# Two reorderings in a 36,612-instruction kernel: weight sums inside a recurrent step, and how an attention's key and value weights are cut into chunks

## The reference, cut to what matters

```
scores = einsum('bhtk,bhsk,bhtsk->bhts', qc, kc, decay)
out    = (qc * exp(b)) @ state + scores @ vc
state  = exp(b_last) * state + (kc * exp(b_last - b)).T @ vc
```

```
kv = (kv_lat @ w_kvb).reshape(T, 6, 128 + 128)
k_nope = rms_norm(kv[..., :128], kn_w);  v = kv[..., 128:]
q_nope = rms_norm(q[..., :128], qn_w);   q_pe = rms_norm(q[..., 128:], ...)
```

## Time and profile before

| | us |
|---|---|
| median of 3 runs | 2535.42 |
| lowest, highest run | 2530.89, 2548.64 |
| profiled execution: its own time | 2550.24 |
| profiled execution: span of the core | 2548.5 |
| mean granted TensorE clock in it | 0.959 of full |
| PE busy | 2434.4 (96%) |
| ACT, DVE, POOL busy | 882.3, 980.6, 932.2 |
| recurrence, round 0 and round 1 (from first scores to last modulation sums) | 139.1 to 236.5, 337.0 to 432.8 |
| stage `kvb` | 1251.9 to 1345.9 |

### The profile page before, as it was taken

The page is one execution under the profiler, slowest core; times in us unless marked ns, Lnnn a source line. Parts: engine busy times, 40 slices in busy tenths (PEclk is TensorE's granted clock), DMA queues, the critical chain, the costliest instruction groups (busy, mean ns, idle before and its releaser), DMA issues.

```text
span 2548.5 us, 36612 instructions
## 1 busy us (share of the span) xinstructions
PE 2434.4 (96%) x14273; PEld 2020.4 (79%) x14273; DVE 980.6 (38%) x1667; ACT 882.3 (35%) x1359; POOL 932.2 (37%) x794
## 2 busy tenths in 40 slices
PE   6999998999999999999999999999999999999997
PEld 3866876988888888888896778888887886688766
DVE  4772673344323223434213235222324004752173
ACT  5433333324222223335212344222344225633462
POOL 2463364233233232334321115444565441135302
PEclk8999899999999999999867999999999999999999
DMA  7177168211222222213100002333332321122211
GB/s 281 59 275 270 50 244 335 63 58 50 66 61 62 66 59 65 66 58 100 43 21 1 1 17 83 99 99 94 95 92 101 109 97 56 52 67 85 71 49 66
DMA packets 56953, 234.94 MB, mean 92 GB/s; under 512 B 6336, under 2 KB 7616, under 8 KB 56064
## 3 DMA queue, kind: packets, MB, share of 16 engines
q1 hardware_dynamic: 56592, 232.45, 27.2%
q0 software_dynamic: 240, 0.79, 0.1%
HBM read 231.11 MB, written 2.10 MB: 92 GB/s over the span
## 4 chain that ended last, share of the span: by engine, by line
PE 82%; DMA 4%; DVE 4%; POOL 3%; ACT 3%; issue 3%; SPq 0%; DVEq 0%; POOLq 0%; ACTq 0%
PE ps L854 15%; PE ps L855 15%; PE ps L856 15%; PE ps L1503 4%; PE ps L1505 4%; PE ps L1506 4%; DMA XB<-ada_dram 4%; PE ps L607 2%; PE ps L1393 2%; POOL w_low L464 2%; PE ps L1319 1%; PE ps L1720 1%; PE ps L1733 1%; PE ps L1657 1%; PE ps L894 1%
## 5 line engine op out<-in xcount | busy, mean ns | idle before, releaser
L464 POOL TENSOR_TENSOR w_low<-ring,w_high 128x512 fp32r<-128x512 f32 (+2 forms) x534 | 696.1, 1326 | 1237.3 <-ACT w_high L455 1228.4
L455 ACT ACTIVATE w_high<-ring 128x1024 fp32r<-128x1024 f32 (+2 forms) x267 | 274.6, 1031 | 973.8 <-PE ps L856 626.2
L854 PE MATMUL ps<-h_high,w_high 128*128 128x512 f32 x1040 | 410.3, 394 | 14.9 <-POOL h_low L717 7.0
L855 PE MATMUL ps<-h_low,w_high 128*128 128x512 f32 x1040 | 407.1, 391 | 0.0
L856 PE MATMUL ps<-h_high,w_low 128*128 128x512 f32 x1040 | 406.4, 391 | 0.0
L854 PEld LDWEIGHTS ps<-h_high,w_high 128*128 128x128 f32 x1040 | 196.6, 189 | 61.9 <-POOL h_low L717 12.9
L856 PEld LDWEIGHTS ps<-h_high,w_low 128*128 128x128 f32 x1040 | 196.4, 189 | 41.6
L855 PEld LDWEIGHTS ps<-h_low,w_high 128*128 128x128 f32 x1040 | 196.8, 189 | 38.3
L1503 PE MATMUL ps<-hidden,w_high 128*128 128x512 f32 (+1 forms) x504 | 178.6, 354 | 0.0
L1505 PE MATMUL ps<-hidden,w_high 128*128 128x512 f32 (+1 forms) x504 | 178.5, 354 | 0.0
L1506 PE MATMUL ps<-hidden,w_low 128*128 128x512 f32 (+1 forms) x504 | 178.3, 354 | 0.0
(11 more groups left out here) (463 smaller groups left out, 5091.3 us busy)
## 6 DMA issues: line engine op xcount, KB each, us to landing
XB<-ada_dram SPq DMA_DIRECT2D x84, 768.0 KB, 6.6
ring<-up_dram SPq DMA_DIRECT2D x88, 512.0 KB, 3.6
ring<-down_dram SPq DMA_DIRECT2D x44, 512.0 KB, 3.6
ring<-winE_dram SPq DMA_DIRECT2D x32, 512.0 KB, 3.3
ring<-win_dram SPq DMA_DIRECT2D x20, 512.0 KB, 3.6
ring<-winC_dram SPq DMA_DIRECT2D x20, 512.0 KB, 3.3
arena<-ada_dram SPq DMA_DIRECT2D x12, 768.0 KB, 20.7
XB<-xl_dram SPq DMA_DIRECT2D x2, 2048.0 KB, 9.1
```

Of the source, the lines that this page charges most:

```text
L455: nc.scalar.activation(WH[p][:, 0:L], RAW[p][:, 0:L], ACT.Copy).then_inc(w_hi, 1)
L464: ins = nc.gpsimd.tensor_tensor(WL[p][:, to], RAW[p][:, to], WH[p][:, to].bitcast(F32), ALU.subtract)
L854: nc.tensor.matmul(bank[:, 0:n], wh[:, cols], hi, start=(k == 0), stop=False)
L855: nc.tensor.matmul(bank[:, 0:n], wh[:, cols], lo, start=False, stop=False)
```

## The change

In the recurrence the order on PE is different. The first two levels of `scores(n)` come first, then `mod_sums(g)`, then levels 2, 3, the transposes and the last level, then `mod_sums(g+1)`, then `outputs(n-1)` directly followed by `updates(n)`, `mod_turn(g-1)` and `mod_sums(g+2)`. The number of instructions is the same.

In stage `kvb` a chunk holds either the keys of two heads or the values of two heads (256 columns for each half of the latent), in turn. For an even h PE does the keys of heads h and h+1 (24 products with 512 or 256 moving tokens); for an odd h it does the values of heads h-1 and h, 36 products with 256 moving columns in place of 72 with 128, two token tiles to a bank. The sums are counted anew (`key_sum`; 7 per pair in place of 8). The means that stood between the token tiles stand all together behind each chunk, the spreads behind them as before. ACT copies four key sums behind each even chunk, DVE three value sums behind each odd one; POOL's waits for the keys follow the new count.

```
--- before.py
+++ after.py
@@ -97,7 +97,7 @@
 
 LAST_SUM = dict(
     win0=lambda k: 2 * k + 1 if k < 6 else 14 + 2 * (k - 7), win1=lambda k: 2 * k + 1 if k < 6 else 14 + 2 * (k - 7),
-    wmlp=lambda k: (1, 3, 6, 6, 9, 9, 11, 13)[k], wout0=lambda k: 2 * k + 1, winM=lambda k: k if k < 5 else 2 * k - 4, qb=lambda k: k, kvb=lambda k: 4 * k + 3,
+    wmlp=lambda k: (1, 3, 6, 6, 9, 9, 11, 13)[k], wout0=lambda k: 2 * k + 1, winM=lambda k: k if k < 5 else 2 * k - 4, qb=lambda k: k, kvb=lambda k: 7 * (k // 2) + (6 if k % 2 else 3),
     woutM=lambda k: k, winE=lambda k: k, woutE=lambda k: 2 * (k - 3) + 1 if k < 6 else k, winC=lambda k: k, woutC=lambda k: k,
 )
 
@@ -106,7 +106,7 @@
     win1=(19, B5), hgS1=(30, B5), hgK1=(13, (5,)), hgU1=(12, (6,)), ro1=(5, (5, 6)),
     wmlp=(14, B5), sv=(8, B8), wout0=(16, B8),
     n1=(4, B8), up0=(88, B8), down0=(12, B8),
-    n2=(4, (5, 6)), n2d=(2, (7, 4)), winM=(11, B5), nlat=(7, (5, 6, 7)), qb=(9, B8), ropek=(1, (7,)), kvb=(24, B5), nqkM=(2, (5,)), nqk=(21, (6, 7)),
+    n2=(4, (5, 6)), n2d=(2, (7, 4)), winM=(11, B5), nlat=(7, (5, 6, 7)), qb=(9, B8), ropek=(1, (7,)), kvb=(21, B5), nqkM=(2, (5,)), nqk=(21, (6, 7)),
     fa=(4, (0, 1, 2, 3)), ropeq=(3, (0, 1, 2)), fb=(2, (3, 4)),
     mS=(24, (0, 2)), mT=(24, (4,)), mV=(6, (6,)), mL=(6, (7,)), woutM=(8, B8),
     n3=(2, (6, 7)), n3d=(2, (4, 5)), up1=(44, (0, 1, 2, 3)), down1=(8, B8),
@@ -857,7 +857,7 @@
                 sums_done(ins, sums, g + i)
             return g + len(segs)
 
-        def split_tokens(pe, stage, c, sums, g, kt, width, m0, src, groups, between=None):
+        def split_tokens(pe, stage, c, sums, g, kt, width, m0, src, groups):
 
             wh, wl = await_parts(pe, stage, c)
             for group in groups:
@@ -870,10 +870,7 @@
                         nc.tensor.matmul(to, hi, wh[:, cols], start=(k == 0), stop=False)
                         nc.tensor.matmul(to, lo, wh[:, cols], start=False, stop=False)
                         ins = nc.tensor.matmul(to, hi, wl[:, cols], start=False, stop=(k == kt - 1))
-                    if t == group[-1]:
-                        sums_done(ins, sums, g)
-                    if between:
-                        between(t)
+                sums_done(ins, sums, g)
                 g += 1
             return g
 
@@ -1096,6 +1093,9 @@
         NM, LSUM, LINV, SKX = carve((2, 4, 2), (2, 4, 2), (2, 4, 2), (2, 4, 2), at=ARENA - 4 * P)
         YM = HL
         qk_hi, qk_lo = sem("qk_hi"), sem("qk_lo")
+
+        def key_sum(h, s):
+            return 7 * (h // 2) + 2 * (h % 2) + s
 
         M_PARTED = [("r", 0), ("k", 0), ("q", 0), ("t", 0), ("k", 1), ("q", 1), ("t", 1), ("k", 2), ("q", 2), ("k", 3), ("q", 3),
                     ("t", 2), ("k", 4), ("q", 4), ("k", 5), ("q", 5)]
@@ -1374,11 +1374,12 @@
                 for c in range(2, 10):
                     win_chunk(r, c)
 
-                def scores(n):
+                def scores(n, levels):
 
                     w = n % 2
-                    pe.wait_ge(hg_ops, 2 * (6 * r + n) + 1)
-                    for l in range(NL + 1):
+                    if levels[0] == 0:
+                        pe.wait_ge(hg_ops, 2 * (6 * r + n) + 1)
+                    for l in levels:
                         if l == NL:
                             pe.wait_ge(hg_ops, 2 * (6 * r + n) + 2)
                             bank = open_bank(pe, SK, keys_sum(n)).rearrange("p (h c t) -> p h c t", h=2, c=2)
@@ -1425,11 +1426,13 @@
                 for n in range(7):
                     g = step_mods(r, n)
                     if n < 6:
-                        scores(n)
+                        scores(n, range(NL // 2))
                     mod_sums(g)
+                    if n < 6:
+                        scores(n, range(NL // 2, NL + 1))
+                    mod_sums(g + 1)
                     if n:
                         outputs(n - 1)
-                    mod_sums(g + 1)
                     if n < 6:
                         updates(n)
                     if n:
@@ -1576,17 +1579,35 @@
             pe.wait_ge(m_tab, 32)
             pe.wait_ge(lat_lo, 4)
             sums_done(nc.tensor.matmul(bank[:, :], C("rot"), M_PE[:, 0, 0:S], start=True, stop=True), "ropek", 0)
-            def mean_behind(h, t):
-                behind = {2: (3, 5), 3: (1, 3, 5), 4: (1, 3, 4, 5)}[len(QK_MEANS[h])]
-                if t in behind:
-                    mean(pe, "nqk", QK_MEANS[h][behind.index(t)])
-
             for h in range(6):
-                g = split_features(pe, "kvb", h, "kvb", 4 * h, 2, 2 * P,
-                                   lambda s, k: (seg_of(KVH, k, s), seg_of(KVL, k, s)), (0, 1))
-                split_tokens(pe, "kvb", h, "kvb", g, 2, 2 * P, P,
-                             lambda t, k: (KVH[:, k, t * P:(t + 1) * P], KVL[:, k, t * P:(t + 1) * P]),
-                             (range(4), range(4, 6)), lambda t: mean_behind(h, t))
+                wh, wl = await_parts(pe, "kvb", h)
+                MM = nc.tensor.matmul
+                if h % 2 == 0:
+                    for j in range(2):
+                        for s, (_, n) in enumerate(SEGS):
+                            bank = open_bank(pe, "kvb", key_sum(h + j, s))[:, 0:n]
+                            for k in range(2):
+                                hi, lo = seg_of(KVH, k, s), seg_of(KVL, k, s)
+                                cols = slice((2 * k + j) * P, (2 * k + j + 1) * P)
+                                MM(bank, wh[:, cols], hi, start=(k == 0), stop=False)
+                                MM(bank, wh[:, cols], lo, start=False, stop=False)
+                                ins = MM(bank, wl[:, cols], hi, start=False, stop=(k == 1))
+                            sums_done(ins, "kvb", key_sum(h + j, s))
+                else:
+                    for t in range(6):
+                        g = 7 * (h // 2) + 4 + t // 2
+                        bank = bank_ap("kvb", g) if t % 2 else open_bank(pe, "kvb", g)
+                        to = bank[:, t % 2 * 2 * P:(t % 2 + 1) * 2 * P]
+                        for k in range(2):
+                            hi, lo = (x[:, k, t * P:(t + 1) * P] for x in (KVH, KVL))
+                            cols = slice(2 * k * P, 2 * (k + 1) * P)
+                            MM(to, hi, wh[:, cols], start=(k == 0), stop=False)
+                            MM(to, lo, wh[:, cols], start=False, stop=False)
+                            ins = MM(to, hi, wl[:, cols], start=False, stop=(k == 1))
+                        if t % 2:
+                            sums_done(ins, "kvb", g)
+                for k in QK_MEANS[h]:
+                    mean(pe, "nqk", k)
                 for k in QK_SPREADS[h]:
                     spread(pe, "nqk", k)
             for k in QK_MEANS[6]:
@@ -2130,9 +2151,10 @@
                 if h == 3:
                     root("nqk", 0)
                 ahead("kvb", h)
-                for s in range(2):
-                    bank = await_sums(act, "kvb", 4 * h + s)
-                    taken(A(seg_of(M_KN, h, s), bank[:, 0:SEGS[s][1]], ACT.Copy), "kvb", 4 * h + s)
+                for x in () if h % 2 else (h, h + 1):
+                    for s in range(2):
+                        bank = await_sums(act, "kvb", key_sum(x, s))
+                        taken(A(seg_of(M_KN, x, s), bank[:, 0:SEGS[s][1]], ACT.Copy), "kvb", key_sum(x, s))
             root("nqk", 1)
             for t in range(4):
                 bank = await_sums(act, "fa", t)
@@ -2368,11 +2390,11 @@
                     for c in range(2, 6):
                         for k in QK_MEANS[c - 2]:
                             if k >= 9:
-                                await_taken(pool, "kvb", 4 * ((k - 9) // 2) + (k - 9) % 2)
+                                await_taken(pool, "kvb", key_sum(*divmod(k - 9, 2)))
                             pool_square("nqk", k, 0)
                         split_lo(stage, c)
                     for k in range(11, 21):
-                        await_taken(pool, "kvb", 4 * ((k - 9) // 2) + (k - 9) % 2)
+                        await_taken(pool, "kvb", key_sum(*divmod(k - 9, 2)))
                         pool_square("nqk", k, 0)
                     for x in range(len(M_PARTED)):
                         whole, high, low_ = m_parts(*M_PARTED[x])
@@ -2773,11 +2795,11 @@
             await_taken(dve, *spread_sum("nlat", 3))
             rotate("ropek", 0, M_PE[:, 0, 0:S], 0)
             for h in range(6):
-                for x, (a, b) in enumerate(((0, 4), (4, 6))):
-                    g = 4 * h + 2 + x
+                for x in range(3 if h % 2 else 0):
+                    g = 7 * (h // 2) + 4 + x
                     bank = await_sums(dve, "kvb", g)
-                    taken(nc.vector.tensor_copy(M_V[:, a:b, h, :],
-                                                bank[:, 0:(b - a) * P].rearrange("p (t n) -> p t n", n=P)), "kvb", g)
+                    taken(nc.vector.tensor_copy(M_V[:, 2 * x:2 * x + 2, h - 1:h + 1, :],
```

(4 more changed lines are left out.)

## The result

| | before | after |
|---|---|---|
| median, runs on the same chip | 2542.53 (9 runs, 2530.89 to 2548.79) | 2511.66 (9 runs, 2504.44 to 2528.35) |
| profiled execution, its span | 2550.24, 2548.5 | 2507.81, 2506.0 |
| mean granted clock in it | 0.959 | 0.980 |
| round 0, round 1 (start of the first scores to start of the last modulation sums) | 97.0, 95.4 | 97.1, 101.3 |
| stage `kvb` | 94.0 | 58.0 |

The medians stand 30.9 us apart. The ratio over all the runs is 0.990, 95% interval 0.987 to 0.993: about 25 us less, 18 to 33. The forecast was 2505 in 2486 to 2525, and 30.5 us less.

The account below looks back on a forecast made before the run. PE, busy in 96% of the span, was taken as the bound. Keys and values 30 us less and recurrence 0.5 less made 30.5 off the 2535.4 median: 2505, with 8 in 10 between 2486 and 2525.

Parts of the forecast that it names:

- the 30 forecast: Stage `kvb`: 94 us down to 64 us, 30 us gained, with four of six chunks starting at half clock.
- 63 and 52: Stage `kvb` at full clock: 63 us before the change and 52 us after.
- The price of a product: Stage `kvb`: starts at full clock 0.11 us apart for 128 columns, 0.12 for 256; values 11 us less.
- dense around the means: Stage `kvb`: dense products surround the means, the argument against rival A; stage 64 us at a clock over 0.8.
- rival A: Stage `kvb`: means behind each chunk, one long pause, keep the clock down; 75 to 88 us, 2516 to 2529; chance 0.27.
- -0.5 forecast: Recurrence, both rounds: -13 + 9 + 1.5 + 2 = -0.5 us, bounds -10 and +8.
- the -13 of "removable" waits for weights: Recurrence: of 20.9 us of PE's waits for modulation weights, 13 would go.
- +9: Recurrence: `updates` directly behind `outputs` waits 1.0 us for DVE's read of bank 6 in ten steps, less 0.8 us.
- +1.5: Recurrence, round 1: a 4.4 us stall for the first block pair delays step 1's chain some 3.5 us; +1.5 net.
- 163.5: Round 0, step 1: the late chain moves DVE's copy to 162.7 and the start of `updates` to 163.5.
- The waits of `updates` in the other steps: Recurrence: a new wait of `updates` for DVE of about 1 us in each step, 4 us in step 1.
- 3.6 us for weights at the start of round 1: Round 1: PE would wait some 4 us for modulation weights at its start.

Follow-up runs that it names:

- e3: After with each values product of 256 columns done as two of 128; 2552.91 us, ratio 1.0065 to before.
- e7: New keys and values, old recurrence order, plus one unused product in PE's wait for DVE's copy ahead of the attention; 2506.02 us, ratio 0.9866 to before.
- e10: e7 with each mean behind a sum or a tile, in place of all behind each chunk; 2506.55 us, ratio 0.9871 to before.
- e4: After with each mean behind a sum or a tile, in place of all behind each chunk; 2512.47 us, ratio 0.9909 to before.
- e8: e7 with scores split in steps 2 to 5 only and two more unused products ahead of the first keys chunk; 2501.41 us, ratio 0.9858 to before.
- e1: After with the recurrence put back to the old order, so keys and values alone; 2515.04 us, ratio 0.9895 to before.

## Why the prediction was right, and where it was wrong

**Keys and values, right in sum and in both terms.** Three profiles of the old stage (94.0, 94.0, 84.3 us) average 90.8, six of the new one with an unfilled start (58.0, 59.2, 63.8, 62.3, 60.9, 58.0) 60.4: 30.4 us less, for the 30 forecast. Content at full clock is 60 against 51 us in before and after (94.0 x 0.64, 58.0 x 0.88), for 63 and 52: the number of products gave about 9 us, not 11. The rest is the clock, some 21 us for 19. The pair on record, 94 to 58, shows 6 us more than the averages: in it before has the slower of its clocks and after the faster. The price of a product held (0.11 us in e3, 0.12 in after), so the row was the right one to go by: e3's content (95.0 x 0.62 = 59 us) is 8 us above after's, where 0.11 us a product gives 11. By the 81 ns of the Trainium skill (TensorE: Matmul & The Clock Gate, "Back-to-back issue gap") it would be 4.5, and the trace, with 0.11 us between starts, doesn't agree.

**The reason given for the clock was half right.** I had "dense around the means" against rival A's "one long pause". By its length rival A didn't come: the six stages with grouped means take 58.0 to 63.8 us and not 75 to 88. In after the 24 means take 2.73 us and no fall stands behind the first three chunks; but in e7 the clock falls in the means behind the first chunk (24 in 3.13 us) and the values start at half clock, so a fall behind such a pause does come in some executions. I credited the layout as a whole; e3 shows that the width of the products carries it, and e10 that a stage without the grouping can be as fast. Neither many short groups of means (e10, clock 0.94) nor few long ones (after, 0.88) kept the clock down, and products of 128 columns without any pause did (e3); e4, at 0.72 with wide products, shows that width doesn't ensure it. The rule of the Trainium skill that stands by rival A (TensorE: Matmul & The Clock Gate, "A second HAM failure mode: psum-queue depth-cycling") is borne out by these traces only in that the clock swings between its levels; in e3 it does so with no pause between the groups (busy 94.97 of 95.00 us).

**The recurrence, wrong: -0.5 forecast, +6.0 measured in the pair on record and about +7 on average.** The term that failed is the -13 of "removable" waits for weights: they fell by 5.6 us in the pair on record and by 6.5 on average (20.4 to 13.8 over six and five profiles). What I added stood: +9 and +1.5 forecast, and the waits for DVE and ACT grew from about 1 to 12.9 us on average. I had seen the DMA idle during the scores and taken that time for recoverable; it is gone from the trace (no window of 1 us in step 1's scores has a DMA share under 0.63 in after, for 0.09 in the earlier trace rows), and the time didn't come back. By the timelines, part of the freed waits turned into waits for the chain, as it starts later, and the rest stayed, as blocks that come late now hold up the scores; only e8 speaks to this by experiment, and it has one profile. In step 1 of round 0 `updates` began at 166.88, as told (163.5, and the round began 3.6 us later), but its wait was 1.51 us and not 4, since PE was itself late by its weights. The waits of `updates` in the other steps, 0.9 us for 1.0, and of 3.6 us for weights at the start of round 1, for some 4, came as told; the half clock behind the seventh step's wait had no term.

**What I had no term for.** The attention's start, 8.9 us in the pair on record. The gain isn't the chunks' (e1, which has them, starts at half clock as before does), and it made up for the recurrence: -30 + 7 - 9 is -32, near the medians' -31, and without the 9 it would be -23. The forecast's nearness owes that much to chance.

## What to carry to other kernels

Where PE is never idle and still slow, read the granted clock by stage, then ask how many columns each product moves: merging two products of 128 columns into one of 256 paid here twice, some 9 us in number and some 21 in clock. An idle DMA is only a gain if what waits for it isn't replaced: before moving a consumer of late data into a producer of a long chain, add what a late block would do to that chain. And one profile of each kernel is not enough for a stage whose clock swings: one instruction order gave 57.7 and 72.4 us.

## What the runs showed of the hardware

- Products of 128 and 256 columns both start 0.21 us apart at half clock (e3; after's first keys chunk), and 0.11 and 0.12 us apart at full: width is nearly free up to 256 here.
- The granted clock can fall with PE busy all the time, if the products are narrow (e3: busy 94.97 of 95.00 us, clock 0.62).
- A pause of 1.4 us stood 1.6 us ahead of a fall of 20 us in four profiles and ahead of none in four others. One unused product of 1.0 us in it cost nothing, and in the one profile that was otherwise like the four (e7) there was no fall.
